# Turning attention probabilities on VectorE instead of TensorE in three looped head groups of a two-layer trunk

## The reference

```
SEQ, D_MODEL, CHUNK, HEAD_DIM, N_HEADS, N_KV_HEADS = 256, 2048, 64, 64, 32, 4
    # q: (B, 4 chunks, 64, 4 kv heads, 8, 64); kb, vb: each chunk's own and its previous chunk's keys, values
    scores = jnp.einsum('bcqkgd,bcjkd->bckgqj', q, kb) * scale
    scores = jnp.where(valid[None, :, None, None, None, :], scores, NEG_INF)
    m = jnp.maximum(jnp.max(scores, axis=-1, keepdims=True), sink)
    p = jnp.exp(scores - m)
    probs = p / (jnp.sum(p, axis=-1, keepdims=True) + jnp.exp(sink - m))
    o = jnp.einsum('bckgqj,bcjkd->bcqkgd', probs, vb)
    o = o.reshape(B, S, Q_WIDTH).astype(h.dtype)
    return o @ w_o
```

## Time and profile before

| | us |
|---|---|
| median of three runs | 1927.6 (1927.12 to 1928.81) |
| the profiled execution | 1927.65 |
| its span in the trace | 1925.7 |
| TensorE busy | 1914.6 (99%) |
| VectorE busy | 1320.4 (69%) |
| ScalarE busy | 962.5 (50%) |

### The profile page before, as it was taken

How to read it: one execution, slowest core, us unless ns; L and a number is a source line. 1 busy time by engine, 2 the same in 40 slices (tenths; PEclk the granted TensorE clock), 3 DMA queues, 4 the chain that set the end, 5 groups by cost and what they waited for, 6 DMA issues and landing times.

```text
span 1925.7 us, 25741 instructions
## 1 busy us (share of the span) xinstructions
PE 1914.6 (99%) x8643; PEld 1576.3 (82%) x8643; DVE 1320.4 (69%) x1819; ACT 962.5 (50%) x1303; POOL 6.2 (0%) x23
## 2 busy tenths in 40 slices
PE   9999999999999999999999999999999999999998
PEld 7777888888888888888888888888888888888886
DVE  6666588647855875686767986787568657846864
ACT  7665465435534543454554444655345435534542
POOL 0000000000000000000000000000000000000000
PEclk9999999999999999999999999999999999999999
DMA  7545556665665666567475565566656666665663
GB/s 244 183 148 178 187 172 202 216 197 174 196 204 181 192 210 196 175 193 231 144 257 174 188 200 196 167 205 219 196 176 190 209 192 188 195 202 169 197 204 109
DMA packets 188677, 368.76 MB, mean 191 GB/s; under 512 B 11434, under 2 KB 11572, under 8 KB 187828
## 3 DMA queue, kind: packets, MB, share of 16 engines
q1 hardware_dynamic: 187264, 360.75, 59.0%
q0 software_dynamic: 1040, 6.82, 1.0%
q10 hardware_dynamic: 292, 0.08, 0.0%
HBM read 365.52 MB, written 2.10 MB: 191 GB/s over the span
## 4 chain that ended last, share of the span: by engine, by line
PE 99%; DMA 0%; DVE 0%; ACT 0%; issue 0%; DVEq 0%; SPq 0%
PE acc L384 17%; PE acc L386 17%; PE acc L385 17%; PE scores L386 15%; PE scores L385 15%; PE scores L384 15%; PE t L409 1%; PE scores L503 0%; PE o L525 0%; PE t L513 0%; PE o L621 0%; DMA h<-in_x 0%; PE t L483 0%; ACT a_hi L671 0%; DVE h L1070 0%
## 5 line engine op out<-in xcount | busy, mean ns | idle before, releaser
L1012 DVE TENSOR_TENSOR w_lo<-w_raw,w_hi 128x1024 fp32r<-128x1024 f32 x680 | 820.4, 1223 | 323.0 <-ACT w_hi L651 305.6
L651 ACT ACTIVATE w_hi<-w_raw 128x1024 fp32r<-128x1024 f32 x680 | 704.3, 1057 | 528.9 <-PE scores L386 211.0
L1043 DVE STREAM_TRANSPOSE work<-s 32x256 f32<-32x256 f32 x544 | 237.3, 436 | 99.9 <-ACT s L794 89.9
L384 PE MATMUL acc<-w_hi,a_hi 128*128 128x512 f32 x768 | 304.1, 396 | 0.1
L386 PE MATMUL acc<-w_hi,a_lo 128*128 128x512 f32 x768 | 299.4, 390 | 0.0
L385 PE MATMUL acc<-w_lo,a_hi 128*128 128x512 f32 x768 | 299.1, 389 | 0.0
L384 PE MATMUL scores<-w_hi,a_hi 128*128 128x512 f32 x672 | 262.2, 390 | 0.0
L386 PE MATMUL scores<-w_hi,a_lo 128*128 128x512 f32 x672 | 261.5, 389 | 0.0
L385 PE MATMUL scores<-w_lo,a_hi 128*128 128x512 f32 x672 | 261.5, 389 | 0.0
L384 PE MATMUL acc<-w_hi,b_hi 128*128 128x512 f32 x640 | 249.8, 390 | 0.0
L384 PE MATMUL scores<-w_hi,b_hi 128*128 128x512 f32 x640 | 249.2, 389 | 0.0
(11 more groups left out here) (144 smaller groups left out, 1386.2 us busy)
## 6 DMA issues: line engine op xcount, KB each, us to landing
w_raw<-in_mlp_w_up SPq DMA_DIRECT2D x256, 512.0 KB, 3.8
w_raw<-in_mlp_w_down SPq DMA_DIRECT2D x256, 512.0 KB, 4.8
w_raw<-in_sgu_w_in SPq DMA_DIRECT2D x64, 512.0 KB, 4.6
w_raw<-in_attn_w_qkv SPq DMA_DIRECT2D x40, 512.0 KB, 4.3
w_raw<-in_attn_w_o SPq DMA_DIRECT2D x32, 512.0 KB, 4.7
w_raw<-in_sgu_w_out SPq DMA_DIRECT2D x32, 512.0 KB, 5.3
gain<-in_norm_gains POOLq DMA_DIRECT2D x4, 1024.0 KB, 6.4
h<-in_x SPq DMA_DIRECT2D x8, 256.0 KB, 6.6
```

The costliest lines, as they stand in the source:

```text
L384: nc.tensor.matmul(bank[t][:, :], lhsT=x_hi[:, kb, tok], rhs=w1, start=(kb == 0), stop=False)
L651: nc.scalar.activation(w_hi[:, i % SLOTS, :], w_raw[:, i % RAW_SLOTS, :], ACT.Copy).then_inc(hi_made, 1)
L1012: nc.vector.tensor_tensor(w_lo[:, i % SLOTS, :], w_raw[:, i % RAW_SLOTS, :], w_hi[:, i % SLOTS, :].bitcast(F32), ALU.subtract).then_inc(lo ...
L1043: last = nc.vector.transpose(turned[:, :, :, src * 32:src * 32 + 32], part[:, :, :, dst * 32:dst * 32 + 32])
```

## The change

In the looped groups TensorE no longer transposes the first half's probabilities. VectorE does it in pieces of 32x32 (turn_p): each instruction takes 32 partitions of probs[0] and writes 32 partitions of pT[0], eight for key rows 0 to 63 (both chunks, 32x256) and eight for key rows 64 to 127 (chunk 1 alone, 32x128). The first eight stand behind split 2, ahead of the second half's normalising, which itself comes ahead of split 3 now; the other eight stand behind split 3. pT[0] lies in yf's free columns, pT[1] where pT lay. ScalarE copies only the second half from PSUM. The products with v of both halves run together behind step (3, 0), half 0 into bank o0, half 1 into o1, and both outputs are split behind the first q_evac and the first rotation. The last group keeps its steps on TensorE, but uses the new places, and VectorE's order of split 3 and the second normalising is changed in it as well.

More of the change, by code:

```diff
@@ L340, in load_row @@
                 pool.dma_start(dst, row.partition_broadcast(P)).then_inc(row_landed[n], 16)
-            pool.wait_ge(pt_filled, 2 * KVH)
+            pool.wait_ge(pt_filled, KVH + 1)
             load_row(0, gain[:, :], gains[0, 1])
@@ L515, in transpose_p, with weigh_half @@
                 last.then_inc(pt_filled, 1)
-            def weigh_v(g, half):
-                pe.wait_ge(pt_copied, g * 2 + (half + 1))
-                at_least(pe, o_lo, g * 2 + half)
+            def weigh_half(half):
                 for i in (1, 0):
@@ L524, in weigh_v, with weigh_both @@
                     for e in range(2):
-                        last = nc.tensor.matmul(ob[i][e * HD:(e + 1) * HD, 0:256], lhsT=v_cur[0:nk, (0, 0, 1, 2)[c], :],
-                                                rhs=pT[0:nk, i, e * 256:(e + 1) * 256], start=True, stop=True)
+                        last = nc.tensor.matmul(ob[half][e * HD:(e + 1) * HD, i * 256:i * 256 + 256],
+                                                lhsT=v_cur[0:nk, (0, 0, 1, 2)[c], :],
+                                                rhs=pT[half][0:nk, i, e * 256:(e + 1) * 256], start=True, stop=True)
                 last.then_inc(o_filled, 1)
+            def weigh_v(g, half):
+                pe.wait_ge(pt_copied, g * 2 + (half + 1) - (KVH - 1))
+                at_least(pe, o_lo, g * 2 + half)
+                weigh_half(half)
+            def weigh_both(g):
+                pe.wait_ge(pt_copied, g + 1)
+                pe.wait_ge(pt_turned, g + 1)
+                at_least(pe, o_lo, g * 2)
+                weigh_half(0)
+                weigh_half(1)
             def attend(blk, g, x_hi, x_lo, in_o=False):
@@ L541, in attend @@
                 if in_o:
+                    steps[1, 1] = [lambda: transpose_p(g, 0)]
+                    steps[2, 0] = [lambda: weigh_v(g, 0)]
                     steps[2, 1] += [lambda: pe.wait_ge(o_lo, 2 * KVH - 1)]
@@ L906, in copy_pT @@
             def copy_pT(g, half):
-                act.wait_ge(pt_filled, g * 2 + (half + 1))
+                if isinstance(g, int):
+                    act.wait_ge(pt_filled, KVH + half)
+                else:
+                    act.wait_ge(pt_filled, g + 1)
                 for i in range(2):
                     nk, _ = keys(2 * half + i)
-                    last = nc.scalar.activation(pT[0:nk, i, :], tb[i][0:nk, :], ACT.Copy)
+                    last = nc.scalar.activation(pT[half][0:nk, i, :], tb[i][0:nk, :], ACT.Copy)
                 last.then_inc(pt_copied, 1)
@@ L926, in attend @@
                 exponentials(g, 1)
-                copy_pT(g, 0)
+                if not evac:
+                    copy_pT(g, 0)
                 split_next(blk, 4)
-                split_o(g, 0)
+                if not evac:
+                    split_o(g, 0)
                 split_next(blk, 5, 6, 7)
@@ L1342, in normalise, with turn_p @@
                 last.then_inc(probs_made, 1)
+            def turn_p(g, dsts):
+                dve.wait_ge(probs_made, g * 2 + 1)
+                for dst in dsts:
+                    for src in range(4):
+                        heads = probs[0][src * 32:src * 32 + 32].rearrange("p b (m n) -> p b m n", n=P)
+                        turned = pT[0][dst * 32:dst * 32 + 32].rearrange("p b (m n) -> p b m n", n=P)
+                        i = slice(0, 2) if dst < 2 else slice(1, 2)
+                        last = nc.vector.transpose(turned[:, i, :, src * 32:src * 32 + 32],
+                                                   heads[:, i, :, dst * 32:dst * 32 + 32])
+                if dsts[-1] == 3:
+                    last.then_inc(pt_turned, 1)
             def split_o(g, half):
@@ L1362, in attend @@
                 row_max(g, 1)
-                split_next(blk, 2, 3)
+                split_next(blk, 2)
+                if evac:
+                    turn_p(g, (0, 1))
                 normalise(g, 1)
+                split_next(blk, 3)
+                if evac:
+                    turn_p(g, (2, 3))
                 split_next(blk, 4)
-                split_o(g, 0)
+                if not evac:
+                    split_o(g, 0)
                 split_next(blk, 5, 6, 7)
```

16 lines of the change are left out of this document (9 added, 7 removed).

## The result

| | before | changed |
|---|---|---|
| median, us | 1927.6 (4 runs, 1927.1 to 1928.8) | 1941.0 (4 runs, 1940.5 to 1944.2) |
| profiled execution, its span | 1927.65, 1925.7 | 1940.47, 1938.7 |

The ratio is 1.0072, interval 1.006 to 1.0084: the change makes the kernel slower by 0.7%. The forecast was 1936.5 and its range ended at 1941; the median, 1941.03, lies just outside it.

The account below looks back on a forecast made before the run. TensorE, busy 99% of the span, was taken as the bound. Three looped groups (+2.44, +2.44, +2.74) and the last (+1.25) sum to 8.87 us on 1927.65, forecasting 1936.5 us; range 1930.5 to 1941.

Parts of the forecast that it names:

- Direction and chain: Attention groups: late w_lo of step 3 delays a slab load, ScalarE's w_hi and copies, then TensorE; slower by 0.46%.
- TensorE's savings: Looped group on TensorE: 0.92 us from eight transposes gone, 0.26 from one entry and exit saved, 1.18 together.
- The turns: VectorE's transposes per looped group: eight of 32x256 take 3.56 us, eight of 32x128 take 2.4 us.
- cheap turns: Rival: the eight 32x256 transposes on VectorE cost at most 0.23 us each, giving 1931.4 us; chance 0.07.
- the cover: Rival: ScalarE's copies do not come behind the late load, TensorE keeps its 3.54 us, giving 1924.1 us; chance 0.12.
- The wait: TensorE ahead of the joint products with v, in each looped group: stands idle 3.62 us until ScalarE's copies end.
- The landing: Load for slab step 7, issued behind w_lo of step 3: lands alone in 3.5 to 3.7 us, 3.9 for w_o.
- The group's 2.44: Net lengthening of a looped group: joint products start 1.31 us later and take 2.15 in place of 1.02.
- the last group's 1.25: Last group: w_lo of step 3 behind the second normalising delays load and copies; last products with v start 1.25 us later.
- The clock: Rival: granted clock falls to 1.2 GHz in TensorE's three waits, 2.7 us each, 8.2 in all, 1944.7 us; chance 0.12.
- GpSimd's gate: Last group: GpSimd's wait on pt_filled at KVH + 1 opens at the same instruction as before and costs nothing.
- the other eight turns: VectorE's eight 32x128 transposes behind w_lo of step 3: end at 111.2, at most 112.4, not the last to come.

Follow-up runs that it names:

- w_lo first: Changed kernel with VectorE's w_lo of step 3 put back directly behind w_lo of step 2, ahead of the turns, in all groups: median 1929.3 us, ratio 1.0004.
- copies first: Changed kernel with ScalarE's copies of the second half's turned probabilities ahead of w_hi of step 7 in looped groups: median 1928.0 us, ratio 1.0005.
- four fillers: Changed kernel plus four matrix products nobody needs, ahead of TensorE's wait for the joint products with v: median 1939.2 us, ratio 1.0062.
- the repeat: Changed kernel run once more, unedited, for its spread: median 1942.4 us, ratio 1.0074; its profiled run took 1939.3 us.
- the kernel without the larger turns: Changed kernel without twelve of its sixteen turns per looped group, only the last four of 32x128 kept, output wrong: median 1934.9 us, ratio 1.004.
- the joint products alone: Kernel before, both halves still transposed on TensorE, with both halves' products with v run together behind step (3, 0): median 1926.8 us, ratio 0.9996.

## Why the prediction was wrong

- **Direction and chain: right.** Slower, by w_lo of step 3 behind the turns, the load behind it, w_hi behind the load, the copies behind w_hi. Undoing the first link (w_lo first) or the last (copies first) takes all three 3 us waits away, each alone.
- **TensorE's savings: right.** 0.92 and 0.26 us a group; measured 0.87 and 0.24.
- **The turns: right.** 3.56 us for eight of 32x256, measured 3.57; 2.4 for eight of 32x128, measured 2.53. The rival of cheap turns is out with that, and so is the cover: w_hi did wait for the load, 4.89 us.
- **The wait: 3.62 us, measured 3.22** in g = 1 (115.32 + 0.23 to 118.77). The largest part of that is the normalising: I took 1.89 us from its start to the next w_lo, and it took 1.65 (110.08 to 111.73). The landing took 3.5 us, not 3.6, and the turns began and ended 0.1 us earlier against the group's start. The group's 2.44 became 2.00, the last group's 1.25 became 0.92. Without the clock the loss is about 2.0 + 2.0 + 2.3 + 0.9 = 7.2 us, not 8.87.
- **The clock: the step that failed.** The sum put it at nothing. It stood among the rivals with a chance of 0.12, for which the prediction gives no reason, and its own rows spoke against so low a chance: the one fall in the trace came 3.35 us behind the last product, and the three waits were put at 3.3 us or more. Two falls came in each profiled run of the changed kernel and cost about 6 us in the first. Nor is one interval what a fall needs: in g = 0 of the changed kernel the clock fell at 83.3 us (a mean of 0.88 over 81 to 84), 2.2 us behind the last product's end (80.67 + 0.39), and with four fillers it fell behind waits of 2.4 us. The price of a fall was 2.7 us forecast, for an assumed twelve slow products; measured were 2.7 to 3.3, and 1.7 in g = 2 of the repeat. With two falls in the forecast and the wait as measured the sum is 7.2 + 6.1 = 13.3; the spans differ by 13.0.
- **The range.** It was said to take in a fall in one or two groups, but two falls of 2.7 us on 1936.5 are 1941.9, beyond its end at 1941. That the median came out at 1941.03, so near that end, is chance: the falls added 6.1 us that the sum did not hold, and the sum was 1.7 us too high without them (8.87 against 7.2). Two smaller slips change nothing: landings of 3.5 to 4.3 us would take off 1.0 or add 2.2, not 0.7 and 2.4, and the rest of the cover and cheap turns together are 0.14, not 0.13.
- The Trainium skill (TensorE: Matmul & The Clock Gate, HAM oscillation) describes a kernel that waits for a load in every step and finds the clock low again behind each wait. The runs agree with it in part: the clock fell at two of three waits of 3.2 to 3.6 us, and at two of three of 2.4 to 2.5.
- **What cheap turns would have given:** the rival's 1931.4 came out at 1930.5 in the run of the kernel without the larger turns whose clock stayed full. Without that condition it did not: the median of that kernel is 1934.9.
- **GpSimd's gate, the other eight turns, the rotations:** cost nothing in the changed kernel, as said. Once the wait was gone, the rotations and the output split came next.

## What to carry to other kernels

Moving work from the limiting engine to one with idle time is priced by what stands behind its new place in that queue, followed to the end: here a write, a slot, a load, another engine's in-order queue, and back. Idle share says nothing about it; the change cost 13 us with the sixteen instructions in one place, and gained 3.6 (0.7 of it from the joint products alone) with them and what follows them in another order. And a new wait of TensorE of some 2 us or more has a second price, the clock behind it: a single fall seen in a trace is no threshold, so put that price in the forecast, not in its tail. Here it was nearly half of the loss.

## What the hardware showed unexpectedly

- The granted clock fell to 1.2 GHz in or behind waits of TensorE of 2.4 to 2.5 us (2 of 3 groups, low for about half as long as in the changed kernel, 1.4 to 1.7 us lost a fall), of 2.6 us (once, 2.0 us behind the last product) and of 3.2 to 3.6 us (2 of 3 groups in each of two traces, 1.7 to 3.3 us lost a fall, once 2.2 us behind the last product); in g = 1 of the changed kernel it did not fall in 3.2 us, in either trace. It can fall behind the wait, when products already run again.
- Turning 32 partitions of fp32 on VectorE in a row costs 0.446 us for 256 elements and 0.316 for 128 (3.57 and 2.53 us for eight): by an estimate from these two, 0.19 us for the instruction and 1 ns for an element. So one instruction of twice the width (0.446) is cheaper than two of the single width (0.632).
